# Routed experts: from one expert per 128-row tile to two experts of 64 rows in one tile

## The reference, cut to what matters

```python
g_idx = top_k(h @ w_rg + b_rg, 1)
top_v, top_i = top_k(logits of the 8 experts of that group, 2)
act = silu(h @ w_gate[e]) * (h @ w_up[e])        # 1024 -> 256, twice
y   = sum over the two experts of weight * (act @ w_down[e])   # 256 -> 1024
```

## Time and profile before

| | |
|---|---|
| median of 3 runs | 3562.57 us (3560.73 to 3563.98) |
| the profiled execution's own time | 3561.31 us |
| its span in the profile | 3559.5 us |
| TensorE busy | 3300.4 us (93%) |
| VectorE busy | 1555.1 us (44%) |
| ScalarE busy | 1020.9 us (29%) |
| GpSimd busy | 345.5 us (10%) |
| moved by DMA | 516.78 MB, 145 GB/s on the mean |
| TensorE's mean granted clock | 0.968 of full speed |

### The profile page before, as it was taken

How to read it: one execution, slowest core, us unless ns; L and a number is a source line. 1 busy time by engine, 2 the same in 40 slices (tenths; PEclk the granted TensorE clock), 3 DMA queues, 4 the chain that set the end, 5 groups by cost and what they waited for, 6 DMA issues and landing times.

```text
span 3559.5 us, 31231 instructions
## 1 busy us (share of the span) xinstructions
PE 3300.4 (93%) x12644; PEld 2106.6 (59%) x12644; DVE 1555.1 (44%) x2783; ACT 1020.9 (29%) x1262; POOL 345.5 (10%) x115
## 2 busy tenths in 40 slices
PE   7899888799986899999979999899999999999998
PEld 3344334444442444444438888777778788888886
DVE  2365482322214443333222888866710244444443
ACT  3524201121103210144123333355542222222222
POOL 0000000000000000000000343322234200000000
PEclk9999998799997999999989999999999999999999
DMA  5123251599971110210022333344543655555551
GB/s 190 48 96 116 96 189 59 188 343 365 368 276 51 36 35 24 71 48 24 24 71 83 139 128 140 129 186 185 201 161 141 204 198 191 191 190 191 191 191 50
DMA packets 276332, 516.78 MB, mean 145 GB/s; under 512 B 10743, under 2 KB 152183, under 8 KB 261656
## 3 DMA queue, kind: packets, MB, share of 16 engines
q1 hardware_dynamic: 240160, 400.05, 32.7%
q10 hardware_dynamic: 29256, 90.03, 6.3%
q0 software_dynamic: 6768, 24.64, 1.8%
HBM read 422.94 MB, written 91.75 MB: 145 GB/s over the span
## 4 chain that ended last, share of the span: by engine, by line
PE 76%; DVE 11%; ACT 9%; issue 2%; DMA 1%; ACTq 0%; DVEq 0%; POOL 0%; SPq 0%
PE P L1898 7%; PE P L1900 7%; PE P L1899 7%; PE P L1478 6%; PE P L1606 6%; PE P L1972 4%; PE P L1974 4%; PE P L1973 3%; PE P L1842 3%; PE P L1555 3%; PE P L1638 3%; PE P L1778 2%; DVE part L402 2%; ACT part L1360 2%; DVE ge L402 2%
## 5 line engine op out<-in xcount | busy, mean ns | idle before, releaser
L1898 PE MATMUL P<-hr,part 128*128 128x512 f32 x1152 | 459.2, 399 | 19.4 <-DVE part L402 19.4
L1899 PE MATMUL P<-hr,part 128*128 128x512 f32 x1152 | 456.1, 396 | 0.0
L1900 PE MATMUL P<-hr,part 128*128 128x512 f32 x1152 | 456.0, 396 | 0.0
L2021 POOL TENSOR_TENSOR part<-raw,part 128x2048 fp32r<-128x2048 f32 x64 | 303.9, 4748 | 1429.0 <-ACT part L1360 1429.0
L1972 PE MATMUL P<-ge,part 128*128 128x512 f32 x1024 | 403.2, 394 | 11.3 <-DVE ge L402 8.6
L1973 PE MATMUL P<-ge,part 128*128 128x512 f32 x1024 | 399.7, 390 | 0.0
L1974 PE MATMUL P<-ge,part 128*128 128x512 f32 x1024 | 399.5, 390 | 0.0
L402 DVE TENSOR_TENSOR part<-raw,part 128x2048 fp32r<-128x2048 f32 x72 | 165.0, 2292 | 371.1 <-ACT part L1360 371.1
L1360 ACT ACTIVATE part<-raw 128x2048 fp32r<-128x2048 f32 x136 | 260.7, 1918 | 107.1 <-PE P L1974 85.8
L1478 PE MATMUL P<-H,W 128*128 128x512 f32 x576 | 256.0, 600 | 6.5 <-DVE H L410 6.5
L1898 PEld LDWEIGHTS P<-hr,part 128*128 128x128 f32 x1152 | 217.1, 188 | 71.0 <-DVE part L402 20.2
(11 more groups left out here) (254 smaller groups left out, 3921.0 us busy)
## 6 DMA issues: line engine op xcount, KB each, us to landing
raw<-in_u SPq DMA_DIRECT2D x64, 1024.0 KB, 4.9
raw<-in_v SPq DMA_DIRECT2D x64, 1024.0 KB, 8.2
W<-in_w_in SPq DMA_DIRECT2D x18, 2048.0 KB, 9.4
W<-in_w_gate SPq DMA_DIRECT2D x32, 1024.0 KB, 7.6
W<-in_w_up SPq DMA_DIRECT2D x32, 1024.0 KB, 11.5
W<-in_w_down SPq DMA_DIRECT2D x32, 1024.0 KB, 11.2
a_scratch<-gt ACTq DMA_DIRECT2D x128, 256.0 KB, 2.4
w_scratch<-window ACTq DMA_DIRECT2D x16, 2048.0 KB, 7.1
```

The lines of the kernel that those rows point to most:

```text
L1898: t.matmul(bank[f % 3], wh[:, k, js], HR[0][:, k, :], start=k == 0, stop=False)
L1899: t.matmul(bank[f % 3], wh[:, k, js], HR[1][:, k, :], start=False, stop=False)
L1900: ins = t.matmul(bank[f % 3], wl[:, k, js], HR[0][:, k, :], start=False, stop=k == 7)
L2021: g.tensor_tensor(out=lo, in0=RAW[n % 3], in1=hi.bitcast(f32), op=SUB).then_inc(s["un_lop"], 1)
```

## The change

Tiles are now pairs of experts. Tile i of `NP = 16` holds expert 2i in rows 0 to 63 and expert 2i+1 in rows 64 to 127. Each matmul of tile_up and down becomes two, one to each half: 64 stationary columns instead of 128, the same 512 moving columns, its own expert's weights, and the upper or lower 64 partitions of the same PSUM bank. So one tile has 16 matmuls of tile_up and 8 of down, each 128x64 by 128x512. The two halves alternate in the order of instructions. Rows beyond 64 of an expert go to overflow tiles of 128 rows, of which there are now `NX_ = 15`; if there is any, all 15 run.

A tile takes three slots: up of both experts, then one down slot with both. Both up slots are released by the tile's tile_up, the down slot by its down step. The `layer_step`s come at each of the first 12 tiles. Seen from one expert, the gathers, the turns, the copies, the activations and the stores of results are halved; the bytes of weights stay.

The router has a few more serial DVE operations (one more threshold for the counts and one for the ranks, a maximum and a multiply-add for the half). Two tables of 32 columns, `half` and `odd`, are added to the parameters. The clearing of the `Yd` rows of overflow tiles moves: no memset, POOL waits for the 12th projection (`pj_mm` 12, the matmul group that ends at 126.8 us) and then writes the constants over them, 15 DMAs of 512 KB; ACT no longer waits for them before its silu at L1161, but only within the overflow branch.

```diff
-        slots.take(("up", 0), 2)
-        slots.drop(("up", 0), s["mu_mm"], 1)
-        for i in range(32):
-            if i + 1 < 32:
-                slots.take(("up", i + 1), 2)
-                slots.drop(("up", i + 1), s["mu_mm"], i + 2)
-            if i % 2 == 0:
-                slots.take(("down", i), 2)
-            else:
-                slots.drop(("down", i - 1), s["md_mm"], 2 * i + 2)
+        for i in range(NP):
+            for e in (2 * i, 2 * i + 1):
+                slots.take(("up", e), 2)
+            slots.take(("down", i), 2)
+            for e in (2 * i, 2 * i + 1):
+                slots.drop(("up", e), s["mu_mm"], i + 1)
+            slots.drop(("down", i), s["md_mm"], 2 * i + 2)
...
             def tile_up(i):
-                w = k8(slot["up", i])
                 pe.wait_ge(s["mi_a"], i + 1)
                 pe.wait_ge(s["mi_v"], i + 1)
                 pe.wait_ge(s["mu_v"], i - 1)
-                pe.wait_ge(*full["up", i])
+                for x in range(2):
+                    pe.wait_ge(*full["up", 2 * i + x])
                 for k in range(8):
-                    ins = t.matmul(bank[2 + i % 2], XT[i % 2][:, k, :], w[:, k, :], start=k == 0, stop=k == 7)
+                    for x in range(2):
+                        xs, w = slice(64 * x, 64 * x + 64), k8(slot["up", 2 * i + x])
+                        ins = t.matmul(bank[2 + i % 2][xs, :], XT[i % 2][:, k, xs], w[:, k, :], start=k == 0, stop=k == 7)
                 ins.then_inc(s["mu_mm"], 1)
...
                     for k in range(2):
-                        ins = t.matmul(bank[5 + c], AV[i % 2][:, k, :], w[:, k, c * 512:(c + 1) * 512], start=k == 0, stop=k == 1)
+                        for x in range(2):
+                            xs, w = slice(64 * x, 64 * x + 64), k2(slot["down", i][:, 2048 * x:2048 * x + 2048])
+                            ins = t.matmul(bank[5 + c][xs, :], AV[i % 2][:, k, xs], w[:, k, c * 512:(c + 1) * 512], start=k == 0, stop=k == 1)
                     ins.then_inc(s["md_mm"], 1)
...
-            rt(ts(OVF, NE, 128.5, None, GT_))
-            rt_wait()
-            rt(stt(OVF, NE, 256.5, OVF, GT_, ADD))
-            rt_wait()
-            rt(stt(OVF, NE, 384.5, OVF, GT_, ADD))
+            rt(ts(OVF, NE, 64.5, None, GT_))
+            for lim in (192.5, 320.5, 448.5):
+                rt_wait()
+                rt(stt(OVF, NE, lim, OVF, GT_, ADD))
...
+            rt(tt(TL, IX, par("odd").unsqueeze(1).broadcast_to([128, 4, 32]), MAX))
...
+            rt(stt(SL, TL, 64.0, SL, MUL, ADD))
...
-            gp.wait_ge(s["z_v"], 1)
-            for i in range(32, NT):
-                nc.gpsimd.dma_start(Yd[i * 128:(i + 1) * 128, :], reg(36, 2)).then_inc(s["zd"], 16)
+            gp.wait_ge(s["const"], 16)
+            gp.wait_ge(s["pj_mm"], 12)
+            for i in range(NP, NT):
+                nc.gpsimd.dma_start(Yd[i * 128:(i + 1) * 128, :], CST[:, :]).then_inc(s["zd"], 16)
```

More of the change, by code:

```diff
@@ L17 @@
                   ("g2", 8), ("gf2", 8), ("gfin", 8), ("qg2", 1), ("kg2", 1), ("hcw", 36), ("hcb", 12),
-                  ("hb1", 1), ("hb2", 1), ("hb3", 1), ("hfr", 1), ("cc", 16)]:
+                  ("hb1", 1), ("hb2", 1), ("hb3", 1), ("hfr", 1), ("cc", 16), ("half", 32), ("odd", 32)]:
     PCOLS[_name] = (_n, _n + _w)
@@ L58 @@
 NOFF = [sum(NORMS[:i]) for i in range(len(NORMS) + 1)]
-NT = 39
+NP, NX_ = 16, 15
+NT = NP + NX_
 SPILL = 32
@@ L173, in program @@
         PF, PU = small(24), small(8).bitcast(u32)
-        LST = small(40).bitcast(u32)[:, 0:NT]
+        LST = small(32).bitcast(u32)[:, 0:NT]
         TIF = small(4)
-        EI = small(7 * 32).rearrange("p (o n) -> p o n", o=7)
-        EF, EU = small(8), small(8).bitcast(u32)
+        EI = small(NX_ * 32).rearrange("p (o n) -> p o n", o=NX_)
+        EF, EU = small(16), small(16).bitcast(u32)
         assert base[0] <= 8 * S
@@ L294, in layer_step @@
         def layer_step(i):
[L296 removed]
+            if i > 11:
                 return None
[L298 removed]
+            n = i
             return ("dma", 0) if n == 0 else ("ctx", 0) if n == 1 else (("mm", "v", "sin")[(n - 2) % 3], (n - 2) // 3) if n < 11 else ("dma", 1)
@@ L601, in vector_program @@
             rt_wait()
-            rt(ts(OVF, NE, 128.5, None, GT_))
-            rt_wait()
-            rt(stt(OVF, NE, 256.5, OVF, GT_, ADD))
-            rt_wait()
-            rt(stt(OVF, NE, 384.5, OVF, GT_, ADD))
+            rt(ts(OVF, NE, 64.5, None, GT_))
+            for lim in (192.5, 320.5, 448.5):
+                rt_wait()
+                rt(stt(OVF, NE, lim, OVF, GT_, ADD))
             rt_wait()
             rt(v.tensor_tensor_scan(out=CUM, data0=ones[:, 0:32], data1=OVF, initial=0.0, op0=MUL, op1=ADD))
[L609 to L614, removed]
+            rt(ts(AA, RK, 63.5, None, GT_))
+            rt(ts(IX, RK, 63.5, None, GT_))
+            for lim in (191.5, 319.5, 447.5):
+                rt_wait()
+                rt(stt(AA, RK, lim, AA, GT_, ADD))
             rt(tt(CU2, CUM, OVF, SUB))
+            rt(tt(TL, IX, par("odd").unsqueeze(1).broadcast_to([128, 4, 32]), MAX))
             rt_wait()
             rt(stt(SL, AA, -128.0, RK, MUL, ADD))
-            rt(stt(CU2, CU2, 31.0, iota[:, 0:32], ADD, SUB))
+            rt(stt(CU2, CU2, NP - 1.0, par("half"), ADD, SUB))
+            rt_wait()
+            rt(stt(SL, TL, 64.0, SL, MUL, ADD))
             rt_wait()
@@ L623, in vector_program @@
             rt_wait()
-            rt(tt(TL, TL, iota[:, 0:32].unsqueeze(1).broadcast_to([128, 4, 32]), ADD))
+            rt(tt(TL, TL, par("half").unsqueeze(1).broadcast_to([128, 4, 32]), ADD))
             rt_wait()
@@ L689, in vector_program @@
             tile_up(0)
-            for i in range(32):
-                if i + 2 < 32:
+            for i in range(NP):
+                if i + 2 < NP:
                     tile_in(i + 2)
@@ L704, in vector_program @@
             dve.wait_ge(s["rt_v"], mark["nx"])
-            more = eng.value_load(NX[0:1, 0:1], min_val=0, max_val=7)
+            more = eng.value_load(NX[0:1, 0:1], min_val=0, max_val=NX_)
             with eng.If(more > 0):
                 x = Port(eng, dve.had)
-                for j in range(7):
+                for j in range(NX_):
                     x.wait_ge(s["xp"], 6 * j + 2)
@@ L717, in vector_program @@
                     v.tensor_copy(YS[0][:, 512:1024], bank[6]).then_inc(s["xv"], 1)
-                x.wait_ge(s["xy"], 112)
-                x.wait_ge(s["xp"], 42)
+                x.wait_ge(s["xy"], 16 * NX_)
+                x.wait_ge(s["xp"], 6 * NX_)
             fl = [0]
@@ L1221, in scalar_program @@
             tile_up(0)
-            for i in range(32):
-                if i + 2 < 32:
+            for i in range(NP):
+                if i + 2 < NP:
                     tile_in(i + 2)
-                if i + 1 < 32:
+                if i + 1 < NP:
                     tile_up(i + 1)
@@ L1240, in scalar_program @@
                 for i in range(3):
-                    x.wait_ge(s[f"ys{i}"], 16 * (11 if i < 2 else 10))
-                for j in range(7):
-                    i = 32 + j
+                    x.wait_ge(s[f"ys{i}"], 16 * (6 if i < 1 else 5))
+                x.wait_ge(s["zd"], 16 * NX_)
+                for j in range(NX_):
+                    i = NP + j
                     x.wait_ge(s["xp"], 6 * j + 1)
@@ L1629, in tensor_program @@
                 turn(SG[i % 2][:, 256:512], bank[4], 2).then_inc(s["mt_mm"], 1)
-                if i + 1 < 32:
+                if i + 1 < NP:
                     tile_up(i + 1)
-                w = k2(slot["down", i - i % 2][:, 2048 * (i % 2):2048 * (i % 2) + 2048])
-                pe.wait_ge(*full["down", i - i % 2])
+                pe.wait_ge(*full["down", i])
                 pe.wait_ge(s["mm_v"], i + 1)
@@ L1643, in tensor_program @@
             pe.wait_ge(s["rt_v"], mark["nx"])
-            more = eng.value_load(NX[0:1, 0:1], min_val=0, max_val=7)
+            more = eng.value_load(NX[0:1, 0:1], min_val=0, max_val=NX_)
             with eng.If(more > 0):
                 x = Port(eng, pe.had)
-                x.wait_ge(s["md_a"], 32)
-                x.wait_ge(s["md_v"], 32)
-                for j in range(7):
+                x.wait_ge(s["md_a"], NP)
+                x.wait_ge(s["md_v"], NP)
+                for j in range(NX_):
                     x.wait_ge(s["xg"], 16 * (j + 1))
@@ L1675, in keys @@
                     pe.wait_ge(s["hm_a"], 8)
-                    pe.wait_ge(s["mi_a"], 32)
-                    pe.wait_ge(s["mi_v"], 32)
+                    pe.wait_ge(s["mi_a"], NP)
+                    pe.wait_ge(s["mi_v"], NP)
                     for k in range(8):
@@ L1685, in keys @@
                 if kind == "cb":
-                    pe.wait_ge(s["mu_v"], 32)
-                    pe.wait_ge(s["md_v"], 32)
+                    pe.wait_ge(s["mu_v"], NP)
+                    pe.wait_ge(s["md_v"], NP)
                     pe.wait_ge(s["cb_v"], 4 * i + 2)
```

(32 more changed lines are left out.)

26 lines of the change are left out of this document (12 added, 14 removed).

## The result

The changed kernel takes 3657.85 us (median of 4 runs, 3656.32 to 3658.30) against 3562.83 us before (median of 4): a ratio of 1.0267, 95% interval 1.0249 to 1.0284, so about 95 us slower. Forecast were 3635 us, range 3595 to 3810, and slower with 0.93.

What follows compares the result with a forecast made beforehand. TensorE was taken to bound the expert stage, DMA close behind. Cycles of 16.3 + 2.5 + 6.87 + 3.43 = 29.1 us, with start, tail and step loads, gave 450.3 against 377.6, +72.7: 3635 us, range 3595 to 3810.

Steps and rivals of the forecast that it cites:

- The release of the slots: Expert stage: a tile's loads wait for the down step two tiles before, so loads and matmuls stand in line; cycle 29.1 us.
- rival A: Expert stage: halves run at once, loads in line with matmuls; 3612 to 3662 us; chance 0.62.
- u and d: Tile_up and down step on TensorE: halves overlap, 6.87 and 3.43 us; 13.74 and 6.87 if one after the other.
- P: Clock cost when TensorE restarts after the wait for weights: 2.5 us a cycle, ends 1.5 and 3.05.
- L: Landing two up loads with a store and a gather beside them: 16.3 us a cycle, ends 13.7 and 18.9.
- Rival B: Expert stage: the two halves don't overlap on TensorE; cycle 39.4 us, +237.5, program 3800 us; chance 0.26.
- the prediction's other way: Two up loads beside store and gather, issued from 860.42: 17.2 us, less 0.8 for late second issue, 16.4.
- Start, tail, step loads: Expert stage outside the cycles: 32.9 us through down(0) including router's 1.2, tail 5.0, step loads 5.
- Behind the stage: After the expert stage everything stays the same; SyncE still waits for the last down.
- Rival F: SyncE's wait before a tile's first up load: DMA queue never runs dry; -48 us, program 3515; chance 0.05.
- Rival O: Overflow branch: all 15 extra tiles run, over 25 us each, near 400 us on top; chance 0.01.

Runs made afterwards that it cites:

- the other dealing of four: Changed kernel, still four weight slots, but two take only up keys and two only down keys: 3605.9 us, ratio 1.0124 to the kernel before.
- the run with the halves in a row: Changed kernel with all eight tile_up matmuls of the first expert, then all eight of the second, instead of alternating: 3739.0 us.
- the kernel of six slots: Changed kernel with six weight slots instead of four in the expert stage, H and eight free arena tiles added: 3491.1 us.
- store and gather held back: Changed kernel, four slots, ACT's tile store and POOL's later gather held until the two awaited up loads have landed: 3613.9 us.
- 14 extra matmuls: Changed kernel with 14 extra f32 matmuls before each tile_up from the third on, while TensorE waits for weights: 3656.3 us.

## Why the prediction was right, and where its sum was short

- **The release of the slots**: as followed. Loads and matmuls are in line; four, five and six slots and the other dealing of four move the time as it says. The result lies in the narrower range of rival A, 3612 to 3662, near its upper end.
- **u and d, the overlap of the halves**: right. 32 instructions in 7.0 to 7.1 us at full clock, 16 in 3.45. The Trainium skill (TensorEngine Tiling (Array Packing), Key Properties) says that tiles run weight loads and matmuls in parallel; the trace agrees, with these 32 and 16 instructions in nearly the time of half as many. The Trainium skill (TensorE: Matmul & The Clock Gate, part 3) gives 2.38x for three column tiles, and the estimate from it was u + d at 13.0 us; measured at full clock are 7.05 + 3.45 = 10.5, and two halves give a factor of 1.95 (2 x 6.87 / 7.05). That the halves overlap was a choice between two ends without a row of this kind, with 0.62 against 0.26, and the run with the halves in a row shows that the alternation makes it. Rival B (3800) is out.
- **P, the clock**: 2.5 taken, 2.47 measured, the mean of tile_up over 14 tiles being 9.34. Of these 2.3 are the clock and 0.2 the 64-wide form, so the match to a hundredth is luck.
- **L, two up loads**: the term that was too small. 16.3 taken, and 0.4 a tile for the step loads; the 14 cycles give 432.8 us in all, 30.9 each, less 9.34 and 3.45 leaves 18.1, 1.5 more in each of 14 cycles, 20.4 us. That is nearly the whole miss of 22.2 in the span (94.9 against 72.7). Two readings were short. The prediction timed the two loads without neighbours until the bytes thin out, 13.7 us, while TensorE waits for the landing, 14.6 us; that is 0.9. And it put the store and the gather at their bytes, 2.6 us, while they cost 3.4; that is 0.8. Together they are 1.7, against 18.0 - 16.3 = 1.7 between the medians. Where the 0.8 goes shows right behind the issue (columns as in the earlier trace rows); first the two loads alone, in the kernel before, then a tile of the changed kernel, whose first load is issued at 849.91:

```profile
520.00:521.00 1.00, 0.00 (x0) 0.00 (x0) 0.96 (x2) 0.00 (x0) 0.00 (x0) 1.00 0.18 13
521.00:522.00 1.00, 0.00 (x0) 0.00 (x0) 0.96 (x2) 0.00 (x0) 0.00 (x0) 1.00 0.73 141
522.00:523.00 1.00, 0.00 (x0) 0.00 (x0) 1.00 (x2) 0.00 (x0) 0.00 (x0) 1.00 1.01 351
...
850.00:851.00 1.00, 1.00 (x4) 0.20 (x3) 0.60 (x1) 0.00 (x0) 0.00 (x0) 1.00 0.01 3
851.00:852.00 1.00, 1.00 (x10) 0.88 (x9) 0.07 (x1) 0.50 (x1) 0.00 (x0) 1.00 0.80 160
852.00:853.00 1.00, 0.12 (x2) 0.00 (x0) 0.96 (x2) 0.10 (x1) 0.83 (x1) 1.00 0.95 296
853.00:854.00 1.00, 0.00 (x0) 0.00 (x0) 0.00 (x0) 0.00 (x0) 0.11 (x1) 1.00 1.04 283
854.00:855.00 1.00, 0.00 (x0) 0.00 (x0) 0.00 (x0) 0.00 (x0) 0.00 (x0) 1.00 0.68 164
```

Against 350 GB/s the loads alone fall short by 0.55 MB in their first microseconds, 1.6 us, and here by 0.84 MB, 2.4 us: 0.8 more. In the prediction's other way, by the pair of loads at 860 us, 17.2 us was measured to the landing, and the 0.8 taken off it brought it near 16.3; that the two ways agreed was luck.

- **Start, tail, step loads**: 31.0 us from the first tile_up to the end of down(0) against 31.7 (the 32.9 without the router's 1.2), as the third up load landed in 9.8 and not 10.5; the tail 4.8 against 5.0; the router's new operations cost 1.0 against 1.2 (from the router's matmul to the one of the lists 46.7 us against 45.7). No delay of ada loads shows at the start: the stage begins 0.5 us earlier than before.
- **Behind the stage** the prediction had nothing, and 4.4 us came: on the chain of waits the gather of results and the load of `dft` behind the last down step take 1.9 us longer together (27.3 against 25.4), and the rest is spread in small pieces. What makes them was not tested.
- **Rival F** was wrong for this kernel and right as a mechanism: where the queue never runs dry, in the kernel of six slots, the program takes 3491 us; the rival had 3515. Its condition, L + P under 13.6, can't be met in the changed kernel, where two loads alone take 14.6.
- **Rival O**: no overflow tile ran; the stores of the stage are 16 (one for each tile).

## What to carry to other kernels

Here halving TensorE's work gained nothing until the transfers that it had covered could start early enough: write down for each load which release it waits for, and which loads stand behind it in the same queue, before counting what the engine saves. With five slots instead of four the changed kernel came out even, with six it gained 71 us, and the room was there in buffers idle during the stage. Time a load from its issue to its landing, since the engine waits for the landing and not for the last bytes. Where a ring serves keys with different lifetimes, a slot of the long-lived kind in the path of the short-lived one costs the difference at each turn (here 3.8 us a tile); dealing the slots out by kind gave 52 us back with no more memory.

## What the runs showed of the hardware that was not expected

- Two f32 matmuls of 128x64 by 128x512 into the two column halves of the array take nearly the time of one of full width, if they alternate: 32 MATMUL instructions in 7.0 to 7.1 us against 16 of full width in 6.87.
- When they do not alternate, TensorE still overlaps the last few instructions of one half with the first of the other, and starts weight loads and matmuls of the following group (882.88 us) ahead of older ones of the other half (883.30 us); tile_up and down together were 2.4 us shorter than their sum.
- Two loads of 2 MB take 14.6 us from issue to landing when nothing is beside them (14.6 also inside the stage, with store and gather held back), and 18.0 with a store and a gather of 0.5 MB each starting beside them: 3.4 us more, where the bytes alone would be 2.6. The last bytes move by 534.0, and the landing is at 534.5.
- With 14 extra matmuls the clock went to half one microsecond after work had begun again, 4.9 us after the last extra matmul, and stayed there for 3.4 us. It bought little: tile_up took 8.4 to 9.9 us in these tiles, against 9.34 on the mean without extra work.
